# Feed-forward up projection as a 2x2 block product with seven block products instead of eight

## The reference

```python
D_MODEL = 1024; SEQ = 1024; D_FF = 2816; FFN_CONV = 3
...
    x = x + mixed @ w_o
    h2 = rms_norm(x, norm2_w)
    gate, up = jnp.split(depthwise_conv_centred(h2 @ w_ffn_up, ffn_conv_w), 2, axis=-1)
    return x + (jax.nn.silu(gate) * up) @ w_ffn_down
```

## Time and profile before

| quantity | value |
|---|---|
| median of three runs | 4085.93 us |
| the profiled execution, its own time | 4090.62 us |
| its span, and mean granted clock of TensorE | 4088.7 us, 0.947 |
| busy in the span: PE, LDWEIGHTS (PEld) | 91%, 75% |
| busy in the span: DVE, ACT, POOL | 40%, 26%, 32% |
| L298, three groups of 2800 matmuls | 962.3, 877.5 and 874.0 us |
| L2055, 88 taps on DVE | 1283 ns each |
| L246 on POOL, 128x1024 | 2519 ns on average |

### The profile page before, as it was taken

The page is one execution under the profiler, slowest core; times in us unless marked ns, Lnnn a source line. Parts: engine busy times, 40 slices in busy tenths (PEclk is TensorE's granted clock), DMA queues, the critical chain, the costliest instruction groups (busy, mean ns, idle before and its releaser), DMA issues. The chain is left out here.

```text
span 4088.7 us, 48340 instructions
## 1 busy us (share of the span) xinstructions
PE 3719.9 (91%) x19184; PEld 3067.0 (75%) x19184; DVE 1636.5 (40%) x2372; ACT 1056.5 (26%) x1805; POOL 1294.9 (32%) x877
## 2 busy tenths in 40 slices
PE   4899999999999999998888999999788978887999
PEld 2677777776898989896776878788676767775777
DVE  8333333343354535452223333333362036655433
ACT  2333333341333333332111111111212013221221
POOL 0312121223221312223343433334332335443443
PEclk7899999999999999998989999999887989998999
DMA  3100000011100000002211111111221111111121
GB/s 128 37 26 32 26 26 26 26 32 39 58 6 17 6 16 1 19 1 72 85 41 37 46 46 51 46 46 46 96 62 46 39 36 44 40 38 38 51 87 67
DMA packets 50862, 172.55 MB, mean 42 GB/s; under 512 B 6152, under 2 KB 12680, under 8 KB 49040
## 3 DMA queue, kind: packets, MB, share of 16 engines
q1 hardware_dynamic: 50704, 170.34, 12.7%
HBM read 150.89 MB, written 19.42 MB: 42 GB/s over the span
## 5 line engine op out<-in xcount | busy, mean ns | idle before, releaser
L298 PE MATMUL DP<-XH,WH 128*128 128x512 f32 x2800 | 962.3, 425 | 101.9 <-POOL WL L246 41.7
L298 PE MATMUL DP<-XL,WH 128*128 128x512 f32 x2800 | 877.5, 395 | 0.0
L298 PE MATMUL DP<-XH,WL 128*128 128x512 f32 x2800 | 874.0, 394 | 0.0
L244 POOL CAST WH<-WRAW 128x1024 fp32r<-128x1024 f32 (+2 forms) x257 | 259.7, 1010 | 1776.9 <-issue 926.7
L298 PEld LDWEIGHTS DP<-XH,WH 128*128 128x128 f32 x2800 | 514.4, 192 | 271.1 <-issue 145.0
L298 PEld LDWEIGHTS DP<-XL,WH 128*128 128x128 f32 x2800 | 534.9, 191 | 116.4
L298 PEld LDWEIGHTS DP<-XH,WL 128*128 128x128 f32 x2800 | 532.5, 190 | 115.8
L246 POOL TENSOR_TENSOR WL<-WRAW,WH 128x1024 fp32r<-128x1024 f32 (+2 forms) x257 | 590.1, 2296 | 20.7
L841 DVE SCALAR_TENSOR_TENSOR SS<-B,RQ,SBI 128x256 f32<-128x256 f32 (+2 forms) x192 | 74.5, 430 | 379.5 <-PE B L546 379.5
L1319 PE MATMUL DP<-PM,XX 128*128 128x64 f32 (+1 forms) x1536 | 171.8, 269 | 15.4 <-ACT XX L1550 15.0
L1319 PEld LDWEIGHTS DP<-PM,XX 128*128 128x128 f32 (+1 forms) x1536 | 162.3, 183 | 29.1 <-issue 26.2
(11 more groups left out here) (439 smaller groups left out, 5381.4 us busy)
## 6 DMA issues: line engine op xcount, KB each, us to landing
WRAW<-in_w_up SPq DMA_DIRECT2D x44, 512.0 KB, 3.5
WRAW<-in_w_attn SPq DMA_DIRECT2D x36, 512.0 KB, 3.6
WRAW<-in_w_down SPq DMA_DIRECT2D x22, 512.0 KB, 3.6
XR<-in_x SPq DMA_DIRECT2D x2, 4096.0 KB, 13.9
WRAW<-in_w_dn SPq DMA_DIRECT2D x16, 512.0 KB, 3.3
WRAW<-in_w_lrux SPq DMA_DIRECT2D x10, 512.0 KB, 3.5
WRAW<-in_w_lrug SPq DMA_DIRECT2D x10, 512.0 KB, 3.5
WRAW<-in_w_bl SPq DMA_DIRECT2D x10, 512.0 KB, 3.2
```

Source lines behind the costliest of these rows:

```text
L244: pool.tensor_copy(WH[b.slot][:, 0:b.kt, :], WRAW[b.slot][:, 0:b.kt, :]).then_inc(w_hi, 1)
L298: mm = pe.matmul(DP[b.slot][:, half * H:half * H + H], w[b.slot][:, k, :], x[:, k, half * H:half * H + H], start=one, stop=end)
```

## The change

The two blocks of a pair (gate `b0`, up `b1`), each cut into its upper and lower 512 inputs, and the activations, cut in the same way and into two halves of the tokens, form a 2x2 block product. Instead of eight products of a quarter (12 matmuls each) seven are made, of combined operands, and their results are added up. This holds for all pairs but the first.

- Activations: four combinations (`XT1` to `XT4`, four tiles of 128x512 each) are made once, in the norm. DVE subtracts (`TN`, 16 operations), ACT rounds, POOL subtracts for the lo part (16 more operations); for these the norm goes through its tiles in the order 0, 4, 1, 5, ... `XT4` is written over the quarter of `XH` and `XL` that only the first pair needs, so it comes after that pair's product.
- Weights: four combinations of 128x512 for each pair, in place in `WRAW`, on POOL, and seven operands of 512 elements (cast and subtraction) in a ring of three (`OPH`, `OPL`); the down blocks go through the same ring by halves. Every step waits for the last one. The buffer of `b0` is given free after the sixth operand, that of `b1` after the seventh.
- Products: seven of 12 matmuls into the four banks of `DP0` and `DP1`; a bank is used again when its sums are done.
- Sums: ACT copies the first product into `GR`, DVE makes seven sums of 512 elements into `GR` and `UR` in SBUF. ACT's copies with the middle tap and DVE's outer taps now read `GR` and `UR` instead of PSUM. `HB` is gone: the product of gate and up goes into `FS`, which lies where `FL` will be, so the multiplication of the even tile stands behind the last addition of the down blocks.

```diff
         TG, TU = at("TG", S0, [P, T]), at("TU", S0 + 4, [P, T])
-        HB = at("HB", S0 + 8, [P, 2, T])
+        GR, UR = at("GR", S0 + 8, [P, T]), at("UR", S0 + 12, [P, T])
         FH, FL = at("FH", S0 + 16, [P, 2, T], F32R), at("FL", S0 + 24, [P, 2, T], F32R)
         FH2, FL2 = at("FH2", S0 + 32, [P, 2, T], F32R), at("FL2", S0 + 40, [P, 2, T], F32R)
+        FS, FS2 = at("FS", S0 + 24, [P, 2, T]), at("FS2", S0 + 40, [P, 2, T])
+        XT1 = [at(f"XT1{i}", 96 + 8 * i, [P, 4, H], F32R) for i in range(2)]
+        XT2 = [at(f"XT2{i}", 112 + 8 * i, [P, 4, H], F32R) for i in range(2)]
+        XT3 = [at(f"XT3{i}", S0 + 32 + 8 * i, [P, 4, H], F32R) for i in range(2)]
+        XT4 = [x[:, 0:4, H:T] for x in (XH, XL)]
+        X11, X21, X22 = ([x[:, a:a + 4, t:t + H] for x in (XH, XL)] for a, t in ((0, 0), (4, 0), (4, H)))
+        MOVING = [X11, XT3, XT2, XT1, X21, X22, XT4]
+        BANK_OF = [[0, 1, 2, 3, 0, 1, 2], [3, 0, 1, 2, 0, 1, 2]]
+        TAKEN = [[None, None, None, None, None, 2, 1], [None, None, None, None, 2, 1, 4]]
...
+        OPH = [at(f"OPH{i}", 136 + 2 * i, [P, 4, P], F32R) for i in range(3)]
+        OPL = [at(f"OPL{i}", 144 + 2 * i, [P, 4, P], F32R) for i in range(3)]
+        OPF = [at(f"OPF{i}", S0 + 20 + 2 * i, [P, 4, P], F32R) for i in range(2)]
...
+        def quarter(pe, hi, lo, moving, dst):
+
+            xh, xl = moving
+            for k in range(4):
+                for w, x, one, end in ((hi, xh, k == 0, False), (hi, xl, False, False), (lo, xh, False, k == 3)):
+                    mm = pe.matmul(dst, w[:, k, :], x[:, k, :], start=one, stop=end)
+            return mm
...
+        def pair_pe(pe, p, q0):
+
+            for j in range(7):
+                if p is PAIR1:
+                    if j == 0:
+                        freed(pe, Block("ffn0", 0, 0))
+                        freed(pe, Block("ffn0", 0, 1))
+                    if j in (1, 6):
+                        pe.wait_ge(flo_ready, 12 if j == 1 else NQ)
+                elif j < 4 and FREED[p.odd][j] is not None:
+                    pe.wait_ge(fw_sum, p.mm + FREED[p.odd][j])
+                if TAKEN[p.odd][j] is not None:
+                    pe.wait_ge(fw_sum, p.mm + TAKEN[p.odd][j])
+                if j == 4 and p.odd == 0:
+                    pe.wait_ge(fc_mid, p.copies)
+                pe.wait_ge(fw_made, p.made + MADE[j])
+                hi, lo = operand(p, j, q0)
+                quarter(pe, hi, lo, MOVING[j], p.bank(j)).then_inc(fw_mm, 1)
+            pe.sem_inc(mm_done, 2)
...
+        def moving_lo(pool, i):
+
+            k, what = i // 3, (XT1, XT3, XT2)[i % 3]
+            pool.wait_ge(fhi_ready, i + 1)
+            pool.tensor_tensor(what[1][:, k, :], TN[k % 2][i % 3][:, :], what[0][:, k, :].bitcast(F32),
+                               ALU.subtract).then_inc(flo_ready, 1)
...
+        def pair_pool(pool, p, q0, free, at_op):
+
+            b0, b1 = WRAW
+            lo, hi = slice(0, 4), slice(4, 8)
+            n = [0]
+
+            def link(ins):
+
+                n[0] += 1
+                ins.then_inc(fw_made, 1)
+                pool.wait_ge(fw_made, p.made + n[0])
+
+            def make(j, src):
+
+                free(j)
+                gate(pool, "pool")
+                oh, ol = operand(p, j, q0)
+                link(pool.tensor_copy(oh[:, :, :], src))
+                link(pool.tensor_tensor(ol[:, :, :], src, oh[:, :, :].bitcast(F32), ALU.subtract))
+                at_op(j)
+
+            pool.wait_ge(w_loaded[0], p.block.loads * 16)
+            make(0, b0[:, lo, :])
+            pool.wait_ge(w_loaded[1], p.second.loads * 16)
+            link(pool.tensor_tensor(b1[:, lo, :], b0[:, lo, :], b1[:, lo, :], ALU.subtract))
+            make(1, b1[:, lo, :])
+            link(pool.tensor_tensor(b1[:, lo, :], b1[:, hi, :], b1[:, lo, :], ALU.subtract))
+            make(2, b1[:, lo, :])
+            link(pool.tensor_tensor(b0[:, lo, :], b1[:, lo, :], b0[:, lo, :], ALU.add))
+            make(3, b0[:, lo, :])
+            make(4, b0[:, hi, :])
+            link(pool.tensor_tensor(b0[:, hi, :], b0[:, hi, :], b1[:, lo, :], ALU.subtract))
+            make(5, b0[:, hi, :])
+            pool.sem_inc(w_hi, 1)
+            pool.sem_inc(w_split, 1)
+            make(6, b1[:, hi, :])
+            pool.sem_inc(w_hi, 1)
+            pool.sem_inc(w_split, 1)
...
+        def ffn_norm_pool(pool):
+            for k in range(4):
+                for j in range(2):
+                    pool.wait_ge(xh_ready, c2.nt + 2 * k + j + 1)
+                    pool.tensor_tensor(XL[:, k + 4 * j, :], NTL[j][:, :], XH[:, k + 4 * j, :].bitcast(F32),
+                                       ALU.subtract).then_inc(nt_used, 1)
+                for i in range(3):
+                    moving_lo(pool, 3 * k + i)
...
+        def ffn_taps(dve, f, t, parts=(0, 1)):
+
+            n = f * 2 + t
+            for part in parts:
+                dst, src = ((TG, GR), (TU, UR))[part]
+                dve.wait_ge(fc_mid, n * 3 + (part + 1))
+                for i, tap in enumerate((0, 2)):
+                    d = dst[:, 1:T] if tap == 0 else dst[:, 0:T - 1]
+                    s = src[:, 0:T - 1] if tap == 0 else src[:, 1:T]
+                    dve.scalar_tensor_tensor(out=d, in0=s, scalar=ffn_tap(f, t, part, tap), in1=d, op0=ALU.mult,
+                                             op1=ALU.add).then_inc(fc_dve, 1)
+                    dve.wait_ge(fc_dve, n * 4 + (2 * part + i + 1))
...
+            dve.wait_ge(fg_silu, n + 1)
+            dve.tensor_tensor(fs[:, t, :], TG[:, :], TU[:, :], ALU.mult).then_inc(fsrc_ready, 1)
...
+        def pair_sums(dve, p, f, t):
+
+            dve.wait_ge(fc_mid, (f * 2 + t) * 3)
+            g0, g1, u0, u1 = GR[:, 0:H], GR[:, H:T], UR[:, 0:H], UR[:, H:T]
+            steps = ((2, 0, g1, g0), (1, 1, u0, g1), (3, 2, u1, u0), (3, 2, g1, g1), (4, 0, g0, g0), (5, 4, g1, g1),
+                     (6, 3, u0, u0))
+            for i, (j, after_sum, dst, x) in enumerate(steps):
+                dve.wait_ge(fw_mm, p.mm + max(j + 1, 3))
+                if after_sum:
+                    dve.wait_ge(fw_sum, p.mm + after_sum)
+                dve.tensor_tensor(dst, x, p.bank(j), ALU.add).then_inc(fw_sum, 1)
+            dve.wait_ge(fw_sum, p.mm + 7)
+            dve.sem_inc(psum_free[0], 1)
+            dve.sem_inc(psum_free[1], 1)
...
+        def ffn_norm_dve(dve):
+            dve.wait_ge(rs_sum, c2.root + 2)
+            for k in range(4):
+                if k:
+                    dve.wait_ge(fsrc_ready, 4 * k)
+                for j in range(2):
+                    dve.wait_ge(nt_used, c2.nt + 2 * k + j - 1)
+                    dve.scalar_tensor_tensor(out=NTL[j][:, :], in0=XR[:, k + 4 * j, :], scalar=col("norm2", k + 4 * j),
+                                             in1=B45[:, :], op0=ALU.mult, op1=ALU.mult).then_inc(nt_ready, 1)
+                if k >= 2:
+                    dve.wait_ge(flo_ready, 3 * (k - 1))
+                t1, t3, t2 = TN[k % 2]
+                dve.wait_ge(nt_ready, c2.nt + 2 * k + 2)
+                dve.tensor_tensor(t1[:, :], NTL[0][:, H:T], NTL[0][:, 0:H], ALU.subtract).then_inc(fsrc_ready, 1)
+                dve.tensor_tensor(t3[:, :], NTL[1][:, H:T], NTL[0][:, H:T], ALU.subtract).then_inc(fsrc_ready, 1)
+                dve.wait_ge(fsrc_ready, 4 * k + 1)
+                dve.tensor_tensor(t2[:, :], NTL[1][:, H:T], t1[:, :], ALU.subtract).then_inc(fsrc_ready, 1)
+                dve.wait_ge(fsrc_ready, 4 * k + 3)
+                dve.tensor_tensor(TN4[k][:, :], NTL[1][:, 0:H], t2[:, :], ALU.subtract).then_inc(fsrc_ready, 1)
...
-                ffn_tile(None, dve, [ffn_block(FLAST, t, i) for i in range(2)], FLAST, t)
+                first, second = Block("ffn", it, 2), Block("ffn", it, 3)
+                pair_sums(dve, in_loop(it, 0), it + 1, 0)
+                ffn_taps(dve, it + 1, 0, (0,))
+                add4(dve, first, it * 2, XR, (0,))
+                ffn_taps(dve, it + 1, 0, (1,))
+                add4(dve, first, it * 2, XR, (1, 2, 3))
+                add4(dve, second, it * 2 + 1, XR, m0=4)
+                ffn_mult(dve, it + 1, 0)
+                pair_sums(dve, in_loop(it, 1), it + 1, 1)
+                ffn_taps(dve, it + 1, 1)
+                ffn_mult(dve, it + 1, 1)
+            pair_sums(dve, TAIL[0], FLAST, 0)
...
```

More of the change, by code:

```diff
@@ L300, in product, with product2 @@
             mm.then_inc(mm_done, 1)
-        def product2(pe, blocks, hi, lo, tiles):
+        def product2(pe, blocks, hi, lo, tiles, order=range(KD)):
             for b in blocks:
@@ new lines, in program, with __init__, bank @@
+        KORDER = [0, 4, 1, 5, 2, 6, 3, 7]
+        MADE = [2, 5, 8, 11, 13, 16, 18]
+        fc_mid, fc_dve, fg_silu, fsrc_ready, fhi_ready, flo_ready = (sem(n) for n in (
+            "fc_mid", "fc_dve", "fg_silu", "fsrc_ready", "fhi_ready", "flo_ready"))
+        fw_made, fw_mm, fw_sum = sem("fw_made"), sem("fw_mm"), sem("fw_sum")
+        class Pair:
```

(33 more changed lines are left out.)

283 lines of the change are left out of this document (183 added, 100 removed).

## The result

The changed kernel takes 4198.69 us (median of 5 runs, 4196.74 to 4236.05), the kernel before 4086.70 us beside it (5 runs, 4085.26 to 4095.61). The ratio is 1.027, 95% interval 1.024 to 1.031: slower by 112 us. The forecast was 4210 (4140 to 4265).

A forecast was written before the change was run, and what follows sets the result against it. PE bounded the kernel before; after the change POOL's chain of operands, lengthened by the lock, would. Terms of 21 + 83 + 20 = 124 us onto the profiled execution gave 4215, set to 4210 us for the median, range 4140 to 4265.

The forecast's parts named there:

- the lock: POOL and DVE: a DVE operation with both inputs in SBUF and a POOL instruction exclude each other for a whole instruction.
- odd pair ends: Loop, pair behind the down product: POOL's seventh operand at 18.1 us, PE ends the pair at 21.5 us.
- nine iterations: Feed-forward loop: each iteration 76.2 instead of 67.0 us, 9.2 us longer, 83 us in nine.
- before the loop: Norm and first combined pair: norm steps of 12.6 us, that pair POOL-bound, 21 us later at the loop.
- after the loop: Two pairs at 30.2 instead of 21.8 us each, plus waits in the down product: 20 us.
- The lock term: POOL's chain in the loop: five DVE operations of 1.23 us with both inputs in SBUF add 6.15 us.
- The combinations: POOL, four weight combinations a pair: 1.28 us each plus a gap of 0.08 us, 1.36 us.
- The second rival: PE's granted clock falls as well in 11 POOL-bound pairs: up to 63 us more, 4273 us; chance 0.15.
- PE's idle time: Sign in the changed stage: PE waits 12 to 15 us an iteration, released by POOL's subtraction for the OPL operands.
- the walk: Summing of one iteration step by step from the down product's end: 76.2 us, or 67.0 without the lock.
- The rival without a lock: POOL's gaps swallow the DVE operations: 67.0 us an iteration, 7 us behind the loop, 4093 us; chance 0.13.
- The rival in which PE bounds: PE stays the bound and the removed matmuls pay: faster, 4039 us; chance 0.05.

The follow-up runs named there:

- e4: Changed kernel with the saved matmuls given back, one block product of each of 20 pairs computed twice; 4202.9 us.
- e5: Changed kernel with POOL's four weight combinations per pair left out, each only a semaphore increment, output not the reference's; 4153.3 us.
- e2: Changed kernel with the middle taps of the tiles falling into the even pair written to PSUM, so DVE's taps and multiplication there have one SBUF input; 4162.1 us.
- e6: Changed kernel with each load of the up projection's raw weights cut from 512 KB to 256 KB, output not the reference's; 4182.1 us.
- e3: Changed kernel with the edits of e1 and e2 together; 4145.7 us.
- e8: e7 with FL of the even pair one product later still, behind the fifth operand, output not the reference's; 4069.4 us.
- e1: Changed kernel with POOL's FL subtraction in the odd pair moved from behind the third operand to behind the fourth; 4189.5 us.
- e9: e3, all combinations kept, with FL of the even pair moved behind the fifth operand; 4160.8 us.
- e7: e3 with POOL's four weight combinations per pair left out, output not the reference's; 4116.7 us.

## Why the prediction was right, and where its sizes were off

The mechanism held: POOL's chain of operands, combinations and FL sets the iteration (PE's waits, e4, e5), the lock adds to it (e2), the load's landing stands on it (e6), and the removed matmuls are worth nothing. That the time came so near is in part luck: the share of the lock was forecast too high and that of everything else too low. The forecast had 76.2 us an iteration with the lock and 67.0 without; measured are 75.3 and, in e2, 71.3. The steps of the forecast, counted from the end of the down product:

| step | forecast | in the profile |
|---|---|---|
| odd pair ends | 21.5 | 23.0 |
| first operand of the even pair | 21.9 | 22.2 |
| its sixth operand | 46.2 | 45.3 |
| pair ends | 51.6 | 51.0 |
| down starts | 52.05 | 51.6 |
| down ends | 76.2 | 75.3 |
| nine iterations | +83 | +74.6 |
| before the loop | +21 | +15.7 |
| after the loop | +20 | +18.8 |

The last three rows divide the 109.2 us of the stage; the loop is taken to begin at the end of the second pair, 64.5 us after the first XL subtraction before and 80.2 us after.

- The lock term, five times 1.23 = 6.15 us, was too large: 4.1 us by the rows, 4.0 us by e2. POOL's instructions grow by 0.70 to 0.87 us, not by the whole DVE operation. POOL's gaps between them hold 0.6 us; the other 1.5 us of the difference the two engines overlap in these rows, and why is open. By the Trainium skill (SBUF — State Buffer, SBUF: two separate sides) the lock is exclusive and the other engine blocks for the whole instruction; the trace agrees that both engines stretch, but by less than that, and that an input in PSUM ends it (e2).
- The combinations, taken at 1.28 + 0.08 us, have a gap of 0.24 us behind them where the next cast reads what they wrote: 1.53 us each. Behind the subtraction of the sixth operand there is a gap of 0.41 us besides. This hid part of the error of the lock term.
- The odd pair ends 1.5 us later than forecast. After PE's idle time of 2.15 us the matmuls come at half pace for a moment, which the sum left out (PE, after):

```profile
2467.67 1.22 PE L2061 MATMUL DP<-XT,OPH 128*128 128x512 f32 x2 [2.15 <-POOL OPL L2232]
2468.69 0.63 PE L2061 MATMUL DP<-XT,OPL 128*128 128x512 f32 x1
2469.12 1.05 PE L2061 MATMUL DP<-XT,OPH 128*128 128x512 f32 x2
```

It moves nothing, because the even pair hangs on the load and POOL: of the eight iterations in this profile four have it, with 23.0 to 23.1 us for the odd pair, and four do not, with 22.1 to 22.5, and all take 75.1 to 75.6. The second rival (63 us for the clock) saw the event and not that PE has time to make it up; the mean granted clock of the window is 0.97.

- PE's idle time was forecast at 12 to 15 us an iteration. In the window it is 73.3 us, 10.7 an iteration, of which 9.0 wait for the OPL subtraction; the rest of what PE loses are matmuls at half pace.
- In the down product PE waits 1.05 us before the fourth output, not 2.4: the taps meet only the third and fourth operand. Before the change PE had waited 1.41 us there, before the third output.
- Before the loop a norm step takes 11.55 us, not 12.6; four steps make 4.2 of the 5.3 us by which this term was too large (POOL, after):

```profile
2173.11 5.12 POOL L2272 TENSOR_TENSOR XL<-NTL,XH 128x1024 fp32r<-128x1024 f32 x2 [10.46 <-ACT XH L2185]
2178.19 5.13 POOL L2172 TENSOR_TENSOR XT<-TN,XT 128x512 fp32r<-128x512 f32 x3
2184.66 2.34 POOL L2272 TENSOR_TENSOR XL<-NTL,XH 128x1024 fp32r<-128x1024 f32 x1 [1.33 <-ACT XH L2185]
```

The sum was 124 us, the measurement 112. The rival without a lock (4093) would have needed taps of 1.23 us and POOL's forms unchanged; the taps of the window have means of 1.73 (TG) and 1.59 us (TU), not the forecast's 2, and the OPL subtractions 1.40. Even e2 and e3, which remove the lock from the even pair, stay at 4162 and 4146 us, so that rival's other half, a 67.0 us iteration from POOL's own work, was wrong too: it is 71.3 in e2. In e3, where FL's wait is gone as well, it is still 70.0; the walk had the gaps too short and the down product without its waits. The rival in which PE bounds (4039) is nearest to e8, and that gave 4069: even then the iteration is 62.8 us and not 61.6, and what the norm and the first pair cost stays.

## What to carry to other kernels

Matmuls saved by a block product are paid on the engine that makes the operands: count that engine's chain per iteration with its gaps, load waits and every operation of its neighbour that has both inputs in SBUF, and compare it with TensorE's time after the saving, not before. An engine busy for a third of the span can become the bound of the stage (here POOL: 32% on the page before, 386 of 517 us in the loop after). When a wait is moved on a full in-order engine, look at what then runs where it used to rest: in e1 0.87 of the 2.26 us went to a neighbour that met it there, and e9 lost time.

## What was not expected of the hardware

- A POOL instruction of 512 elements is stretched by 0.83 to 0.87 us (a cast by 0.70) beside one DVE operation of 1.23 us with both inputs in SBUF; the DVE operation at its side takes 1.3 to 2.1 us. With one DVE input in PSUM both have their own lengths.
- A wait of PE of 2.84 us was followed by some eight matmuls at 0.43 us in every iteration of e7; one of 2.46 to 2.49 us at the same place in e9 in five iterations of eight. A longer wait need not be: in the profile after, one of 2.15 us in the odd pair was, one of 2.97 us in the even pair was not (0.23 us a matmul behind it). What tells them apart stays open.

```profile
2414.80 0.73 PE L2061 MATMUL DP<-XT,OPH 128*128 128x512 f32 x2 [2.97 <-POOL OPL L2232]
2415.37 0.39 PE L2061 MATMUL DP<-XT,OPL 128*128 128x512 f32 x1
```

- The gap between two linked POOL steps is 0.08 us behind a cast, 0.24 us behind a combination and 0.41 to 0.42 us behind a subtraction where two bare semaphore increments stand between.
